# Norms of one half of the tokens beside the products of the other half, in a two-layer encoder step on one core

## The reference, cut to what matters

```
x = layer_norm(ALPHA * x + mix @ w_out, ln_mix_g, ln_mix_b)
f = (silu(gate) * val) @ w_down      # gate, val = conv3(x @ w_up)
x = layer_norm(ALPHA * x + f, ln_ffn_g, ln_ffn_b)
x = x + sigmoid(x @ ple_w_gate + ple_b_gate) * (p @ ple_w_proj)
```

## Time and profile before

| what | us |
|---|---|
| median of 3 runs (lowest, highest) | 4039.81 (4038.9, 4042.9) |
| the profiled execution's own time | 4039.59 |
| span in its profile | 4037.8 |
| PE busy | 3603.0 (89%) |
| DVE busy | 1857.6 (46%) |
| POOL busy | 1195.3 (30%) |
| ACT busy | 1028.2 (25%) |

### The profile page before, as it was taken

The page is one execution under the profiler, slowest core; times in us unless marked ns, Lnnn a source line. Parts: engine busy times, 40 slices in busy tenths (PEclk is TensorE's granted clock), DMA queues, the critical chain, the costliest instruction groups (busy, mean ns, idle before and its releaser), DMA issues. The chain is left out here.

```text
span 4037.8 us, 74421 instructions
## 1 busy us (share of the span) xinstructions
PE 3603.0 (89%) x31490; PEld 3420.7 (85%) x31490; DVE 1857.6 (46%) x2270; ACT 1028.2 (25%) x1395; POOL 1195.3 (30%) x574
## 2 busy tenths in 40 slices
PE   8998887979999999898997876777688999999988
PEld 7997786969999999798996445777678999999978
DVE  1653554255454454744412225545445554544563
ACT  2454333032111111221013334222322111111131
POOL 3333432333333333343332000000043333333342
PEclk9998998989999999999998988998899999999999
DMA  3111001001111111112211016121200111111101
GB/s 123 57 50 50 1 0 72 31 21 45 44 42 42 47 42 42 43 36 98 92 66 46 1 61 197 35 42 27 103 31 32 42 46 42 42 42 47 53 22 68
DMA packets 99768, 203.89 MB, mean 50 GB/s; under 512 B 57824, under 2 KB 59104, under 8 KB 98464
## 3 DMA queue, kind: packets, MB, share of 16 engines
q1 hardware_dynamic: 92528, 160.26, 12.3%
q10 hardware_dynamic: 7088, 41.33, 2.6%
HBM read 164.34 MB, written 37.23 MB: 50 GB/s over the span
## 5 line engine op out<-in xcount | busy, mean ns | idle before, releaser
L712 PE MATMUL PS<-XH,WHI 128*128 128x274 f32 x5248 | 1531.7, 292 | 93.8 <-DVE XL L2052 31.7
L712 PE MATMUL PS<-XL,WHI 128*128 128x274 f32 x5248 | 1529.6, 291 | 0.0
L712 PE MATMUL PS<-XH,WLO 128*128 128x274 f32 x5248 | 1526.9, 291 | 0.0
L801 POOL TENSOR_TENSOR WHI<-RAW,EPS 128x1024 fp32r<-128x1024 f32 x218 | 417.4, 1915 | 2470.4 <-PE PS L712 2428.9
L712 PEld LDWEIGHTS PS<-XH,WHI 128*128 128x128 f32 x5248 | 999.6, 190 | 100.0 <-issue 48.5
L712 PEld LDWEIGHTS PS<-XL,WHI 128*128 128x128 f32 x5248 | 1001.6, 191 | 0.0
L712 PEld LDWEIGHTS PS<-XH,WLO 128*128 128x128 f32 x5248 | 1000.6, 191 | 0.0
L804 POOL TENSOR_TENSOR WLO<-RAW,WHI 128x1024 fp32r<-128x1024 f32 x218 | 569.5, 2612 | 17.1
L712 PE MATMUL PS<-HH,WHI 128*128 128x274 f32 x1408 | 410.9, 292 | 15.3 <-DVE HL L2077 13.1
L712 PE MATMUL PS<-HH,WLO 128*128 128x274 f32 x1408 | 408.6, 290 | 0.0
L712 PE MATMUL PS<-HL,WHI 128*128 128x274 f32 x1408 | 407.6, 290 | 0.0
(11 more groups left out here) (399 smaller groups left out, 4648.1 us busy)
## 6 DMA issues: line engine op xcount, KB each, us to landing
RAW<-in_units SPq DMA_DIRECT2D x218, 512.0 KB, 3.2
prepared_rows<-PREP SPq DMA_DIRECT2D x8, 1096.0 KB, 5.6
CIN<-prepared_rows SPq DMA_DIRECT2D x17, 512.0 KB, 5.3
c_rows<-DX ACTq DMA_DIRECT2D x14, 548.0 KB, 2.8
RKV<-c_rows SPq DMA_DIRECT2D x4, 1644.0 KB, 9.9
X<-in_x SPq DMA_DIRECT2D x8, 548.0 KB, 9.0
XR<-in_x ACTq DMA_DIRECT2D x1, 4384.0 KB, 18.4
x_rows<-Y ACTq DMA_DIRECT2D x1, 4384.0 KB, 12.9
```

The source lines that it names most:

```text
L712: last = nc.tensor.matmul(PS[:, 4 * slot + b, 0:width], wt[:, ring, w], r[:, k, b * width:(b + 1) * width], start=n == 0, stop=n == 3 * nk ...
L801: nc.gpsimd.tensor_tensor(WHI[:, s, :], RAW[:, s, :], ZERO.to_broadcast([128, 1024]), ALU.add)\
```

## The change

For each layer norm the 1,096 columns are taken as two halves of 548, h = 0 and h = 1, and PE, DVE and ACT get a new hand-written order.

- w_out and group 0's up units stand twice in the list of units, 24 more units in all (218 become 242). A pass over one half (`matmul_half`, two blocks of 274, 48 matmuls) needs the whole unit again. Out stage: 8 half units for h = 0, then 8 for h = 1 with h = 0's norm beside them. Then 4 half up units of h = 0, with h = 1's norm beside them, then 4 of h = 1. The first of these (`matmul_half_rows`) goes k-tile by k-tile, waiting for each XL tile.
- The last down group and the embedding products go in 16 half steps each. The embedding products no longer wait for the root; the first two gate units go half by half.
- The squares are added up on DVE (`add_square`), so PE does 2 matmuls for a variance instead of 16. Gain and inverse root are applied in one DVE instruction (`scaled`), the bias on ACT, in two Identity instructions (`high`). All of XL is made on DVE (`lower`); POOL does nothing but split weights.
- The last gate unit is released in halves, and XH and XL of the next layer are made half by half; the projection's first unit goes by k-tiles. Y leaves in nine transfers, XR comes in eight.
- `clear_sum` is gone; the gap columns of Y are zeroed too.

```diff
+        def duo(n):
+            return PS[:, 2 * n:2 * n + 2, 0:BW]
+        def squares(n, h):
+            x = SQUARES[0 if n % 2 == 1 and h == 0 else 1]
+            return row_half(x[:, 1, :] if n % 2 == 1 and h == 0 else x[:, 0, :], h), \
+                [row_half(x[:, 0, :] if n % 2 == 1 and h == 0 else x[:, 1, :], j) for j in range(2)]
...
+        def matmul_half(place, ring, first, nk, hi, lo, h, middle=None):
+            for b in range(2):
+                if b and middle:
+                    middle()
...
+        def matmul_half_rows(place, ring, nk, hi, lo, h, row_ready):
+            for k in range(nk):
+                row_ready(k)
...
# PE, layer_end
-                        matmul_unit(s, s, 0, 8, XH, XL).then_inc(unit_done, 1)
-                pe.wait_ge(out_read, 10 + 10 * l)
-                norm_sums(2 * l)
+                        matmul_half(s, s, 0, 8, XH, XL, 0).then_inc(unit_done, 1)
+                for m in range(8):
+                    pe.wait_ge(unit_split, first + 8 + m + 1)
+                    pe.wait_ge(out_read, 8 + m + 1 + 18 * l)
+                    middle = {0: lambda: mean(2 * l, 0), 3: lambda: variance(2 * l, 0)}.get(m)
+                    matmul_half(m % 2, m % 2, 0, 8, XH, XL, 1, middle).then_inc(unit_done, 1)
                 pe.wait_ge(gaps_zeroed, 1 + 2 * l)
...
+                    middle = {0: lambda: mean(2 * l, 1), 2: lambda: variance(2 * l, 1)}.get(t)
+                    matmul_half(t % 2, t % 2, 0, 8, XH, XL, 0, middle).then_inc(unit_done, 1)
...
+                        matmul_half_rows(2, 0, 8, XH, XL, 1, lambda k: pe.wait_ge(ln_lo, 8 + k + 1 + 32 * l))\
+                            .then_inc(unit_done, 1)
...
+                    if q == 9:
+                        pe.wait_ge(down_read, 82 + 98 * l)
+                        mean(2 * l + 1, 0)
...
+                    matmul_half(q % 2, m // 4, 256 * (m % 4), 2, PH, PL, h)\
+                        .then_inc(unit_done if q % 8 == 7 else ple_done, 1)
+                    if q == 1:
+                        mean(2 * l + 1, 1)
+                    if q == 6:
+                        variance(2 * l + 1, 0)
+                    if q == 15:
+                        variance(2 * l + 1, 1)
...
# ACT
-            act.dma_start(XR[:, :, :], io["x"]).then_inc(x_back, 16)
+            for k in range(8):
+                act.dma_start(XR[:, k, :], io["x"][:, k, :]).then_inc(x_in[k // 2], 16)
...
+            def high(n, h, k):
+                act.wait_ge(ln_scaled, 16 * n + 8 * h + k + 1)
+                nc.scalar.activation(row_half(XH[:, k, :], h), y, ACT.Identity, bias=b)
+                nc.scalar.activation(y, y, ACT.Identity, bias=b).then_inc(ln_hi, 1)
...
# ACT, FFN norm, n = 2 * l + 1
+                for k in range(8):
+                    square(n, 1, k)
+                    projected(8 + k)
+                for k in range(8):
+                    high(n, 0, k)
+                log(n, 1)
+                root(n, 1)
...
# DVE, mix norm, n = 2 * l
+                for m in range(8):
+                    add_mixed(l, 0, m)
+                centre_rows(n, 0, 0, 2)
+                add_mixed(l, 1, 0)
+                centre_rows(n, 0, 2, 6)
+                add_mixed(l, 1, 1)
+                centre_rows(n, 0, 6, 8)
+                add_mixed(l, 1, 2)
+                add_mixed(l, 1, 3)
+                norm_rows(n, 0, 0, 2)
+                add_mixed(l, 1, 4)
+                norm_rows(n, 0, 2, 5)
+                add_mixed(l, 1, 5)
+                norm_rows(n, 0, 5, 8)
+                add_mixed(l, 1, 6)
+                add_mixed(l, 1, 7)
+                centre_rows(n, 1, 0, 8)
+                norm_rows(n, 1, 0, 8)
...
# DVE, FFN norm
+                centre_rows(n, 0, 0, 8)
+                centre_rows(n, 1, 0, 8)
+                norm_rows(n, 0, 0, 8)
+                norm_rows(n, 1, 0, 8)
```

More of the change, by code:

```diff
@@ L99, in lay_out @@
             full(a["w_in0"][:, first + 128 * m:first + 128 * m + 128])
-    full(a["w_out0"])
+    for half in range(2):
+        full(a["w_out0"])
     ffn(0)
@@ L116, in lay_out @@
     units.append(np.ascontiguousarray(v.reshape(2, 128, 512).transpose(1, 0, 2).reshape(128, 1024)))
-    full(a["w_out1"])
+    for half in range(2):
+        full(a["w_out1"])
     ffn(1)
@@ L1580, in chunk, with square, log @@
-            def chunk(l, g, unit, first=False):
+            def square(n, h, k):
+                act.wait_ge(ln_sub, 16 * n + 8 * h + k + 1)
+                total, through = squares(n, h)
+                if k >= 3:
+                    act.wait_ge(ln_squares, 14 * n + 7 * h + k - 2)
+                nc.scalar.activation(through[(k - 1) % 2] if k else total, row_half(Y[:, k, :], h), ACT.Square)\
+                  .then_inc(ln_sq, 1)
+            def log(n, h):
+                act.wait_ge(ln_var, 2 * n + h + 1)
+                step(nc.scalar.activation(rows(row_half(RS, h)), duo(2 + h), ACT.Ln, bias=EPS[:, 0:1], scale=1 / 1024))
@@ new lines, in layer_end @@
+                n = 2 * l + 1
+                for k in range(6):
+                    square(n, 0, k)
+                    projected(k)
+                square(n, 0, 6)
+                square(n, 0, 7)
+                projected(6)
+                log(n, 0)
+                projected(7)
+                root(n, 0)
+                for k in range(8):
+                    square(n, 1, k)
+                    projected(8 + k)
+                for k in range(8):
+                    high(n, 0, k)
@@ new lines, in layer_end @@
+                log(n, 1)
+                root(n, 1)
+                for k in range(8):
+                    high(n, 1, k)
+                for m in range(7):
+                    act.wait_ge(unit_done, m + first + 91)
+                    act.wait_ge(gate_added, m + 1 + 11 * l)
+                    nc.scalar.activation(rows(SG[m % 2][:, :]), banks(m % 2), ACT.Sigmoid, bias=col("ple_b%d" % l, m))\
+                      .then_inc(gate_read, 1)
+                    if m:
+                        act.wait_ge(gate_added, m + 2 + 11 * l)
+                        act.dma_start(out[:, m - 1, :], Y[:, m - 1, :]).then_inc(out_done, 16)
@@ new lines, in add_square, with centre_rows @@
+            def add_square(n, h, k):
+                total, through = squares(n, h)
+                dve.wait_ge(ln_sq, 16 * n + 8 * h + k + 1)
+                if k >= 2:
+                    dve.wait_ge(ln_squares, 14 * n + 7 * h + k - 1)
+                nc.vector.tensor_tensor(total, total, through[(k - 1) % 2], ALU.add).then_inc(ln_squares, 1)
+            def centre_rows(n, h, first, last):
+                for k in range(first, last):
+                    centred(n, h, k)
+                    if k >= 3:
+                        add_square(n, h, k - 2)
+                if last == 8:
+                    add_square(n, h, 6)
+                    add_square(n, h, 7)
@@ new lines, in norm_rows, with sum_up @@
+            def norm_rows(n, h, first, last):
+                for k in range(first, last):
+                    scaled(n, h, k)
+                    if k >= 2:
+                        lower(n, h, k - 2)
+                if last == 8:
+                    lower(n, h, 6)
+                    lower(n, h, 7)
+                    if h == 0:
+                        gaps(ln_lo, 16 * n + 8, gaps_zeroed)
+            def sum_up(n, h, m):
+                y, total = row_half(Y[:, m, :], h), row_half(YSUM[n % 2], h)
+                if m == 1:
+                    nc.vector.tensor_tensor(total, row_half(Y[:, 0, :], h), y, ALU.add).then_inc(ln_total, 1)
+                elif m > 1:
+                    dve.wait_ge(ln_total, 14 * n + 7 * h + m - 1)
+                    nc.vector.tensor_tensor(total, total, y, ALU.add).then_inc(ln_total, 1)
@@ L2078, in low, with add_down @@
                 last.then_inc(h_done, 1)
-            def add_down(l, g, unit, tiles=range(8), first=False, last=False):
+            def add_down(l, g, unit, tiles=range(8), first=False):
                 for m in tiles:
@@ L2140, in layer_end @@
                 step.leave(9)
-                dve.wait_ge(down_read, 82 + 90 * l)
-                clear_sum(2 * l + 1)
-                add_down(l, 10, first + 72, range(0, 5), last=True)
+                for q in range(5):
+                    add_last(l, q)
                 dve.wait_ge(p_hi, 1 + l)
```

488 lines of the change are left out of this document (262 added, 226 removed).

## The result

The changed kernel takes 3950.95 us (median of 4 runs, 3945.34 to 3955.89), beside 4041.36 us for the kernel before on the same chip; the ratio is 0.9776, 95% interval 0.9759 to 0.9793. The forecast was 3945, the range 3895 to 3988. The profiled execution took 3948.91 us with a span of 3947.1, 90.7 us less than the span before.

The account below looks back on a forecast made before the run. PE, busy 89% of the span, was taken as the bound, with 220 us of losses in reach; gains of 2 x 18.4 + 2 x 17.5 + 14.2 + 11.5 - 3 = 94.5 from 4039.6 gave 3945 us, range 3895 to 3988.

Parts of the forecast that it names:

- The lock: DVE instructions with two SBUF inputs wait for POOL's split under way to end, some 2.1 us each by the lock alone.
- Mix norm: Out stage to first up units, both layers: 34.7 us still lost against 53.1, a gain of 18.4 each.
- FFN norm: Last down product to first gate units, both layers: loss falls from 40.6 to 23.1 us, a gain of 17.5 each.
- Boundary: Layer 0's last gate unit to layer 1's projection: 1.5 of 15.7 us stays lost, a gain of 14.2.
- End: After the last matmul: 5.6 us remain of 17.1, a gain of 11.5.
- XR: Loading XR in eight transfers puts seven more issues on ACT's queue before the squares; loss 3 us, layer 0 only.
- At nothing: Parts priced at zero: 24 more units hidden behind PE, RAW loads, Y's gaps, missing clear_sum, group 0's later convolution.
- rival 4: POOL becomes the bound of the 48 half units, 8.5 us a cycle, 115 lost: 4060 us; chance 0.03.
- decision point of 8.1: POOL's cycle in us from which the kernel would come out slower because POOL bounds the half units.
- Rival 1: The lock waits hide: gain up to 169 us, 3871; half of that relief gives 3905; chance 0.23.
- Rival 2: Lock waits are twice those walked: gain 39 us in all, 4000; chance 0.13.
- Rival 3: DVE's written order undoes the overlap altogether; only boundary and end pay, 4017 us; chance 0.05.

Follow-up runs that it names:

- run 3: Changed kernel with POOL splitting only 128 of each unit's 1,024 columns from layer 0's out stage on, leaving out work; 3877.54 us in one run.
- Run 7: Changed kernel with POOL's WHI and WLO of a unit each written in two instructions of 512 columns from layer 0's out stage on; 3928.18 us, ratio 0.9728.
- run 2: Changed kernel with DVE's and ACT's tiles of the two halves interleaved in the FFN norms; 3945.41 us, ratio 0.9769.
- run 6: Changed kernel with the FFN norms' half tiles interleaved on DVE and ACT, and their bias added on DVE instead of ACT; 3941.78 us, ratio 0.9759.
- Run 1: Changed kernel with ACT giving in1_read its first two counts before layer 0's end stage instead of after it; 3939.53 us, ratio 0.9754.
- Run 8: Changed kernel with POOL writing WHI twice for every unit from layer 0's out stage on; 4057.5 us in one run.
- Run 4: Changed kernel with the mix norm's first variance at half unit 4 instead of 3, and XR's issues after the mixer's last XH copy; 3931.76 us, ratio 0.9737.

## Why the prediction held, step by step

**The lock.** Shown by run 3: DVE instructions with two SBUF inputs are slower beside POOL's splits (1.42 and 1.58 us against 0.80 and 0.73), those with an input from PSUM are not (0.72), and PE's stalls go with the splits. Run 7 shows that the longest wait shrinks with the length of POOL's instructions, from 2.95 to 1.83 us for a half tile, the sum of waits much less. The rows in order of time agree: additions of 1.8, 2.2 and 2.95 us stand in the out stage, none over 0.8 in the embedding products, where POOL's only splits fall beside none of them. The Trainium skill, SBUF — State Buffer, "Who interferes with whom", has the rule for two SBUF inputs, and the trace agrees with it. The reading was too narrow, though: copies of two columns with one SBUF input wait too (up to 2.35 us, 0.22 on average in run 3), and so did a half tile of TENSOR_SCALAR with one SBUF input in the kernel before (0.55 us where POOL was idle, 1.58 beside POOL's XL). The prediction priced neither.

**Mix norm** (18.4 predicted, 22.3 and 20.2 measured). The places were right. Stall at the variance of h = 0: 4.0 predicted, 3.58 measured, with 7.8 us of lock waits in the eight two-input instructions before it where 9.0 were walked. Tile 5 and gaps: 7.3, measured 1.17 + 5.47. Variance of h = 1: 4.4, measured 3.64. First unit of h = 1: 8.4, measured 4.3, so this term was half as large; which part of the walk was too long there was not looked for. The remaining loss (restarts, means, variances) is 53.1 - 22.3 - 18.2 = 12.6 against the 10.6 walked.

**FFN norm** (17.5 predicted, 14.1 and 12.9 measured). The idle time before the gates was 14.25 instead of 12.6: the first two `scaled` took 2.42 and 2.87 us, since both instructions of one gate unit's split fell on just them. To this come small waits between the half products (1.62, 1.05, 0.61, 1.33, 0.77, 0.50), of which the walk had 1.5. Together they are more than the miss of 3.4 and 4.6, so something else was shorter than walked. The reason given, `norm_rows` queued behind `add_square`, was the visible one but not the limit: with the queue mended (run 2) DVE's 2.7 us a tile (run 6) and ACT's, an estimated 2.4, took its place. The table loads were priced rightly: 1.28 us each, with under 0.02 of idle time before a load that follows another instruction.

**Boundary** (14.2 predicted, 8.3 measured). This is the step that failed. It read "h = 1's follow PE's rows", and left out that PE's first unit there waits for `in1_read` too, which ACT gives behind all its copies. The working followed the data (XH, XL) and not the credits. Run 1 gave back 6.0, and that is the whole miss.

**End** 11.5 came out as worked out, to the tenth, which is luck at this closeness. **XR** looks right (3 predicted, 2.7 by the clock time of the out stage's start), but the seven more issues cost 4.3 us, as the count from ACT's store issue shows; 1.5 us of faster matmuls before them hid the difference. The 4.10 us that they took on ACT's queue (4.70 for eight against 0.60) lay in the range given, 2.4 to 4.2, of which the sum took 3.

**At nothing.** The 24 more units were hidden, with 1.35 us to spare in a cycle of 6.1. Run 8 took that cover away and landed at 4057.5. That this is close to rival 4's 4060 is chance: the cycle was 7.5 and not 8.5, and most of the loss came by DVE. For the same reason rival 4's decision point of 8.1 was too far out: it counted only the half units' cycles, while the longer splits also stretch DVE's waits and slow the full units (773 matmuls instead of 788 between 1100 and 1200).

**Rivals.** Rival 1 needs locks that hide; run 3 shows what that would have given, 3878. Rival 2 fell: DVE waits at most once for each POOL instruction, as walked. Rival 3 was true only in small: moving the variance mends what DVE's order cost. Rival 1's half-way point is slightly off as added up: 94.5 and half of the other 74.5 give 3908, not 3905. The forecast's sum was 3.8 us above the span's gain of 90.7. That flatters it, and in part it was luck: without the 4.1 of the rest the terms measure 86.6 against 94.5, with the boundary 5.9 and the FFN norms 8.0 short and the mix norms 5.7 over.

## What to carry to other kernels

When a vector instruction is moved beside another engine's stream that makes it wait, price it at its duration there, and look at all its forms, the small one-input copies too. Where a wait lasts a whole instruction, cutting the other engine's long instructions in two is a cheap mend (some 16 us here by its stretches) until that engine becomes the bound; expect less than half of the waits to go, since there are now twice as many instructions to meet. When a hand-over is made earlier, list every semaphore that the consumer waits for, credits too, and ask where in its engine's queue each is given. When mending a stage with two nearly level engines, expect nothing from the first mend and judge only both together.

## What the runs showed of the hardware

- Run 4 took 5.2 and 3.1 us of stalls away and gained 8.1 and 5.7. Behind the wait of 5.47 us PE ran at a granted clock of 0.77 (832.40 to 841.30 in the changed kernel, where its 52 matmuls fill 8.90 us), between the levels of 1.2 and 2.4 GHz; behind the wait of 1.17 it ran at 1.00 (820.60 to 829.40). So the number of long stalls matters beside their sum.
- A loop of 64 x 64 matmuls that no edit touches took 318.7 to 330.7 us in 14 profiled executions, and the whole second mixer 1004.6 to 1013.5 in nine kernels with the same code for it. The cause was not looked for.
- Eight issues of 548 KB transfers in a row took ACT's queue 4.70 us (0.59 each) in the changed kernel and 4.16 (0.52 each) in run 4, the single issues of the stores 0.33 to 0.36.
- A copy of 128 x 2 elements between SBUF tiles took DVE at most 0.37 us in run 3, 1.26 in run 7 and 2.35 in the changed kernel, the longer the POOL instructions beside it.
